# A second norm's factors brought in by TensorE with a diagonal matrix, and VectorE's boundary work in another order

## The reference

```python
def rms_norm(x, g):
    xf = x.astype(jnp.float32)
    y = xf * lax.rsqrt(jnp.mean(xf * xf, -1, keepdims=True) + EPS)
    return (y * g.astype(jnp.float32)).astype(x.dtype)

h = h + rms_norm(a, norm_g[i, 1])              # the first norm: of the block's result
f = conv_ffn(rms_norm(h, norm_g[i, 2]), ...)   # the second norm: ahead of the next block
h = h + rms_norm(f, norm_g[i, 3])
```

## Time and profile before

| | |
|---|---|
| median of three runs | 1113.65 us |
| profiled execution | 1116.95 us |
| its span | 1114.8 us |
| mean granted TensorE clock in it | 0.987 of full speed |
| TensorE matmul busy | 1056.9 us (95%) |
| VectorE busy | 681.1 us (61%) |
| ScalarE busy | 561.8 us (50%) |
| GpSimd busy | 412.9 us (37%) |

### The profile page before, as it was taken

How to read it: one execution, slowest core, us unless ns; L and a number is a source line. 1 busy time by engine, 2 the same in 40 slices (tenths; PEclk the granted TensorE clock), 3 DMA queues, 4 the chain that set the end, 5 groups by cost and what they waited for, 6 DMA issues and landing times.

```text
span 1114.8 us, 21844 instructions
## 1 busy us (share of the span) xinstructions
PE 1056.9 (95%) x8226; PEld 963.6 (86%) x8226; DVE 681.1 (61%) x1079; ACT 561.8 (50%) x1022; POOL 412.9 (37%) x283
## 2 busy tenths in 40 slices
PE   9799999999999998899999997799999999999997
PEld 7699689999978997699999967688888889999996
DVE  3555767767666656667767654567677545544444
ACT  4445565555555555465555545334434255544442
POOL 1000233343341332233343354555645355534331
PEclk9999999999999999999999998899999999999999
DMA  8234466566534442466556432133312334536551
GB/s 332 78 126 127 146 205 191 184 193 192 184 114 133 151 151 76 153 207 193 186 186 195 166 114 95 49 105 96 96 58 77 114 104 160 154 114 222 183 177 38
DMA packets 46135, 162.27 MB, mean 146 GB/s; under 512 B 5248, under 2 KB 5504, under 8 KB 45952
## 3 DMA queue, kind: packets, MB, share of 16 engines
q1 hardware_dynamic: 44784, 156.79, 43.2%
q0 software_dynamic: 1296, 4.72, 1.3%
HBM read 160.44 MB, written 1.05 MB: 145 GB/s over the span
## 4 chain that ended last, share of the span: by engine, by line
PE 83%; DVE 8%; POOL 3%; ACT 3%; issue 2%; DMA 1%; DVEq 0%; POOLq 0%; SPq 0%; ACTq 0%
PE work L388 13%; PE work L390 13%; PE work L389 13%; PE work L1590 6%; PE acc L388 5%; PE acc L389 5%; PE acc L390 5%; PE work L2299 4%; PE work L2311 2%; PE acc L2311 2%; PE acc L1839 1%; POOL low L357 1%; PE acc L1853 1%; ACT high L346 1%; PE acc L1855 1%
## 5 line engine op out<-in xcount | busy, mean ns | idle before, releaser
L357 POOL TENSOR_TENSOR low<-raw,high 128x1024 fp32r<-128x1024 f32 x109 | 264.2, 2426 | 328.9 <-ACT high L346 328.9
L357 DVE TENSOR_TENSOR low<-raw,high 128x1024 fp32r<-128x1024 f32 (+3 forms) x183 | 272.7, 1497 | 165.3 <-ACT high L346 165.2
L346 ACT ACTIVATE high<-raw 128x1024 fp32r<-128x1024 f32 (+2 forms) x293 | 300.0, 1032 | 49.3 <-DMA raw<-in_w_out 23.5
L388 PE MATMUL work<-xh,high 128*128 128x256 f32 (+1 forms) x1032 | 292.6, 283 | 0.7 <-DVE low L357 0.7
L389 PE MATMUL work<-xl,high 128*128 128x256 f32 (+1 forms) x1032 | 289.5, 280 | 0.0
L390 PE MATMUL work<-xh,low 128*128 128x256 f32 (+1 forms) x1032 | 289.0, 280 | 0.0
L388 PEld LDWEIGHTS work<-xh,high 128*128 128x128 f32 (+1 forms) x1032 | 194.6, 189 | 7.7 <-issue 4.8
L389 PEld LDWEIGHTS work<-xl,high 128*128 128x128 f32 (+1 forms) x1032 | 194.9, 189 | 2.4 <-issue 0.7
L390 PEld LDWEIGHTS work<-xh,low 128*128 128x128 f32 (+1 forms) x1032 | 194.7, 189 | 0.2
L1113 POOL TENSOR_TENSOR h<-gelu,cv 128x256 f32<-128x256 f32 x44 | 48.8, 1109 | 200.5 <-ACT gelu L1033 106.7
L1590 PE MATMUL work<-xh,high 128*128 128x256 f32 x256 | 79.1, 309 | 9.5 <-DVE silu L1639 9.5
(11 more groups left out here) (383 smaller groups left out, 2230.0 us busy)
## 6 DMA issues: line engine op xcount, KB each, us to landing
raw<-in_w_ffn SPq DMA_DIRECT2D x132, 512.0 KB, 4.3
raw<-in_w_out SPq DMA_DIRECT2D x39, 512.0 KB, 4.2
raw<-in_w_diff SPq DMA_DIRECT2D x32, 512.0 KB, 4.1
raw<-in_w_att SPq DMA_DIRECT2D x32, 512.0 KB, 3.7
raw<-in_w_gdn SPq DMA_DIRECT2D x24, 512.0 KB, 4.0
raw<-in_w_mla SPq DMA_DIRECT2D x8, 512.0 KB, 3.5
raw<-in_w_gdnz SPq DMA_DIRECT2D x8, 512.0 KB, 3.6
raw<-in_w_mla SPq DMA_DIRECT2D x8, 384.0 KB, 3.2
```

The costliest lines, as they stand in the source:

```text
L346: act.activation(high[k][:, 0:w], raw[k][:, 0:w], ACT.Copy).then_inc(high_done[k], 1)
L357: eng.tensor_tensor(low[k][:, 0:w], raw[k][:, 0:w], high[k][:, 0:w], ALU.subtract).then_inc(low_done[k], 1)
L388: pe.matmul(out, lhs[0], rhs[0], start=start, stop=False)
```

## The change

A new tensor `diag` holds, for each tile, a 128x128 matrix with the second norm's roots on the diagonal. ScalarE makes it from the identity (`pre_diag`), with the root as the scale of each row. VectorE's multiply into `hn` takes the gain alone (`pre_gained`), so it waits for `hid` and no longer for the root. TensorE multiplies `hn` by `diag` instead of transposing by the identity, which gives the transposed and scaled half at once; it takes half 0 of both tiles first, then half 1, and runs six idle products ahead instead of seven. The splits follow that order. The squares of `hid` go to `xl`. On VectorE the first norm's work stands in another order, too. At the program's beginning nothing changes.

```diff
     def pre_pe(pe, n):
         pe.wait_ge(g["const"], 48)
-        spin(pe, W[3][:], 7)
-        for t in range(NT):
-            for half in range(2):
-                pe.wait_ge(n_["hn"], 4 * (n - 1) + 2 * t + half + 1)
+        spin(pe, W[3][:], 6)
+        for half in range(2):
+            for t in range(NT):
+                pe.wait_ge(n_["hn"], 4 * (n - 1) + 2 * half + t + 1)
+                if half == 0:
+                    pe.wait_ge(n_["diag"], 2 * (n - 1) + t + 1)
                 for b in range(4):
                     at = (4 * half + b) * P
-                    last = pe.transpose(work[:, 2 * t + half, b * P:(b + 1) * P], hn[:, t, at:at + P], ident)
+                    last = pe.matmul(work[:, 2 * t + half, b * P:(b + 1) * P], hn[:, t, at:at + P], diag[:, t, :],
+                                     start=True, stop=True)
                 last.then_inc(n_["turned"], 1)
...
+    def pre_diag(act, n, t):
+        act.wait_ge(n_["root"], 2 * n + t + 1)
+        act.activation(diag[:, t, :], ident, ACT.Copy, scale=stat[:, 8 + t:9 + t]).then_inc(n_["diag"], 1)
...
-    def pre_norm(dve, n, t, half):
-        dve.wait_ge(n_["root"], 2 * n + t + 1)
+    def pre_gained(dve, n, t, half):
+        dve.wait_ge(n_["hid"], 4 * (n - 1) + 2 * t + half + 1)
...
-        dve.scalar_tensor_tensor(hn[:, t, c], hid[:, t, c], stat[:, 8 + t:9 + t], pre_gain[:, c], ALU.mult,
-                                 ALU.mult).then_inc(n_["hn"], 1)
+        dve.tensor_tensor(hn[:, t, c], hid[:, t, c], pre_gain[:, c], ALU.mult).then_inc(n_["hn"], 1)
...
     def post_dve(dve, n, p, k):
-        for t in range(NT):
-            post_gained(dve, n, t, p, k)
-            if t == 0:
-                post_mean(dve, n, 0)
-        for half in range(2):
-            post_add(dve, n, 0, half)
+        post_gained(dve, n, 0, p, k)
+        post_mean(dve, n, 0)
+        post_add(dve, n, 0, 0)
+        post_gained(dve, n, 1, p, k)
         post_mean(dve, n, 1)
+        post_add(dve, n, 0, 1)
         for half in range(2):
             post_add(dve, n, 1, half)
-            if n < 4 and half == 0:
-                pre_mean(dve, n + 1, 0)
 
     def pre_act(act, n):
         for t in range(NT):
             pre_square(act, n, t)
+        for t in range(NT):
+            pre_diag(act, n, t)
...
+    def pre_dve(dve, n):
+        pre_mean(dve, n, 0)
+        pre_gained(dve, n, 0, 0)
+        pre_mean(dve, n, 1)
+        pre_gained(dve, n, 1, 0)
         for t in range(NT):
-            pre_split_act(act, n, t)
-
-    def pre_dve(dve, n):
-        pre_norm(dve, n, 0, 0)
-        pre_mean(dve, n, 1)
-        pre_norm(dve, n, 0, 1)
-        for half in range(2):
-            pre_norm(dve, n, 1, half)
+            pre_gained(dve, n, t, 1)
```

More of the change, by code:

```diff
@@ L461, in build @@
     g = sems("g", "x second_x const")
-    n_ = sems("n", "hid sq mean root hn turned xh xl gain")
+    n_ = sems("n", "hid sq mean root diag hn turned xh xl gain")
+    diag = sb("diag", [P, NT, P])
     h = sems("h", "qkev s mx sm e p pt ptev vev pv oh ol rope roped turned turned_ev")
@@ L517, in pre_square, with pre_split_act @@
             c = cols(half)
-            act.activation(hn[:, t, c], hid[:, t, c], ACT.Square, scale=1 / 32,
+            at = 4 * t + 2 * half
+            out = xl[:, at:at + 2, :].rearrange("p b k -> p (b k)") if n else hn[:, t, c]
+            act.activation(out, hid[:, t, c], ACT.Square, scale=1 / 32,
                            accum_out=stat[:, 16 + 2 * t + half:17 + 2 * t + half]).then_inc(n_["sq"], 1)
-    def pre_split_act(act, n, t):
-        for half in range(2):
-            act.wait_ge(n_["turned"], 4 * n + 2 * t + half + 1)
-            act.activation(x_part(xh, t, half), turned(t, half), ACT.Copy).then_inc(n_["xh"], 1)
+    def pre_diag(act, n, t):
+        act.wait_ge(n_["root"], 2 * n + t + 1)
+        act.activation(diag[:, t, :], ident, ACT.Copy, scale=stat[:, 8 + t:9 + t]).then_inc(n_["diag"], 1)
+    def pre_split_act(act, n, t, half):
+        act.wait_ge(n_["turned"], 4 * n + (2 * half + t if n else 2 * t + half) + 1)
+        act.activation(x_part(xh, t, half), turned(t, half), ACT.Copy).then_inc(n_["xh"], 1)
     def pre_mean(dve, n, t):
@@ L541, in pre_split_dve @@
             for t in range(NT):
-                dve.wait_ge(n_["xh"], 4 * n + 2 * t + half + 1)
+                dve.wait_ge(n_["xh"], 4 * n + 2 * half + t + 1)
                 dve.tensor_tensor(x_part(xl, t, half), turned(t, half), x_part(xh, t, half),
@@ L612, in pre_act @@
             pre_square(act, n, t)
+        for t in range(NT):
+            pre_diag(act, n, t)
     def pre_act_split(act, n):
-        for t in range(NT):
-            pre_split_act(act, n, t)
-    def pre_dve(dve, n):
-        pre_norm(dve, n, 0, 0)
-        pre_mean(dve, n, 1)
-        pre_norm(dve, n, 0, 1)
-        for half in range(2):
-            pre_norm(dve, n, 1, half)
+        for half in range(2):
+            for t in range(NT):
+                pre_split_act(act, n, t, half)
+    def pre_dve(dve, n):
[3 more added lines that the diff above has]
+        pre_gained(dve, n, 1, 0)
+        for t in range(NT):
+            pre_gained(dve, n, t, 1)
     def boundary_act(act, n, p, k):
@@ L682, in start_act @@
         for t in range(NT):
-            pre_split_act(act, 0, t)
+            for half in range(2):
+                pre_split_act(act, 0, t, half)
         act.wait_ge(g["const"], 16)
```

## The result

The changed kernel took 1123.86 us (median of five runs, 1123.36 to 1127.13), the kernel before beside it 1115.82. The ratio over all runs is 1.0083, 95% interval 1.0070 to 1.0096: slower, by 9.3 us (the two medians lie 8.0 apart). In what follows a figure in us behind a ratio is the ratio times the median of the kernel before that ran beside it. The profiled execution took 1125.76 us with a span of 1123.6, against 1116.95 and 1114.8 before.

A forecast was written before the change was run, and what follows sets the result against it. TensorE was taken as the bound, with the change touching only four block boundaries and the last norm. Delays of 6.8 us plus 3.3 for clock falls, together 10.1, on a median of 1113.65 gave 1123.8 us; range 1118 to 1128.5.

The forecast's parts named there:

- The last add 0.71 later: First norm, first boundary: in the new order VectorE's last add ends 0.71 us later than before.
- The diagonal: Second norm, ScalarE: the 128x128 copy with a scale read per row takes 0.35 us.
- The groups: TensorE, in place of transposes: float32 products of two records, 0.23 us each, 0.92 us a group of four.
- Tile 1's multiply by the gain: VectorE, second norm: it waits for the first power and ends about 129.1; the second power ends at 129.5.
- Behind the groups: TensorE: first real product 1.00 us behind the idle product's start, as before; the changed half and tile order brings nothing.
- The sign of the 11 us: Boundaries: forecast wrong if the first real product comes less than 11 us behind the first add.
- The boundary at full clock: Four boundaries and program's end, delays alone: +1.68, +2.05, +0.56, +1.71 and +0.84, sum 6.8 us.
- The clock: TensorE's longer waits: clock falls in first and second boundary, 1.4 us each, fourth +0.5; 3.3 us.
- The total: Whole program: 6.8 us of delays and 3.3 of clock, together 10.1; median 1123.8 us; chance 0.62.
- the clock that holds: Rival, boundaries: TensorE is fast enough behind the wait; delay alone, +6 us, 1119.7 to 1120.5; chance 0.22.
- The cheap product: Rival, TensorE's groups: a product costs as little as a transpose, 0.5 us a group; no change; chance 0.05.
- the dear one: Rival, TensorE's groups: each 0.8 us more, +12 us on the delays; 1129 to 1133 us; chance 0.08.

The follow-up runs named there:

- mean_early_no_last: Kernel before with the first norm's second mean ahead of tile 0's adds, nine idle products in the fourth boundary, none behind the transposes: ratio 0.9977.
- after_spins: Changed kernel with 8, 9, 8 and 10 idle products ahead of the first group in the four boundaries, not 6: 1120.99 us, ratio 1.0060.
- order_alone: Kernel before with VectorE's new order of the first norm alone, second norm and transposes as before: 1120.47 us, ratio 1.0046.
- plain_products: Kernel before with true float32 products with the identity instead of transposes, waits and orders as before: ratio 1.0040, 4.5 us slower.
- mean_early: Kernel before with the first norm's second mean ahead of both adds of tile 0, not behind them: 1111.50 us, ratio 0.9960.

## Why the prediction was right, step by step

- **The last add 0.71 later.** Forecast 7.28 from the first gain to the last add's end; measured 7.29. The wait for the first power, the order behind it and the power that ends 0.41 behind an overlapping add came as worked out.
- **The diagonal.** Taken at 0.35, measured 0.40. The prediction's nearest row was an activation out of PSUM; a nearer one was in the same trace, of an activation from SBUF that reads a value per row too:

```profile
L2444 ACT ACTIVATE causal_prob<-causal_prob,soft 128x128 f32<-128x128 f32 x8 | 3.2, 403 | 24.2 <-DVE soft L2525 24.2
```

- **The groups.** Forecast 0.92 each, measured 0.89, in 32 records. The Trainium skill's factor of four for transpose mode ("TensorE: Matmul & The Clock Gate", "Terms") doesn't hold for start to start here: two records of 0.114 a product, against 0.145 at most for a transpose.
- **Tile 1's multiply by the gain.** The prediction lets it wait for the first power. In the kernel it waits for `hid` alone, and the three behind the second mean ran in a row from 127.82. The second power ended 9.30 behind the first gain, against 9.45 forecast.
- **Behind the groups.** The prediction took 1.00 from the idle product to the first real one, as before, and nothing for the new order of halves. From the start of the idle product to the second real product it was 1.19 before (131.01 to 132.20) and is 0.98 now (132.26 to 133.24). The 1.00 held a wait for `xl` of half 0 (mean_early_no_last), and that wait is gone: VectorE ends its last multiply earlier against the groups, and half 0 of both tiles is turned first. How much each of the two does isn't shown. This term was put at nothing and is worth 0.2 us in the first boundary, which is what separates the +1.68 forecast there from the 1.49 measured; the other differences cancel.
- **The sign of the 11 us.** The first real product was to come 11 us or more behind the first add. By its record it comes at 132.72, 10.73 behind 121.99, which is under the bound. By the end of the idle product (132.26 + 0.86 = 133.12) it is 11.13, against 11.24 forecast. I read it by the second, since its successor begins at 133.24; the bound was too near the forecast to decide anything.
- **The boundary at full clock.** Forecast +1.68, +2.05, +0.56, +1.71 and +0.84, 6.8 in all. after_spins, where the clock held, has +1.48, +1.87, +0.81, +0.71 and +0.85, 5.7; the fourth is taken against a boundary that itself had a fall (1.2 or so), without which it is +1.9, and the sum 6.9. The +0.56 of the third was wrong: it took a late product of tile 1 for a property of the kernel, and it was one of that execution. The wait ahead of its groups was 1.87 and not 1.3.
- **The clock.** Forecast were three falls of 1.4, one each in B0, B1 and B3. Three came, of 1.4 each, but one in B1 (1.42) and two in a row in B3 (2.86), and none in B0, though the wait there was 2.54 and as long as forecast (2.4). By places the forecast with the clock was 3.1, 3.5, 0.6, 2.2 and 0.8, and measured were 1.5, 3.3, 0.9, 3.6 and 0.9: the sum came out by errors on both sides, which is luck. The length of the wait ahead of the groups doesn't decide it. In these profiles no fall followed waits of 2.54 and 1.87 (B0 and B2 after), of 1.74 (B1 of order_alone) and of 1.91 (B3 of plain_products), and a fall followed 2.94, 3.11, 3.14 and 4.34, but also 1.90 (before) and 1.38 (mean_early).
- **The total.** 10.1 forecast on the execution; the places give 10.1, the span 8.8, the runs 9.3 (7.8 to 10.7). That the median, 1123.86, fell on the 1123.8 forecast is luck: the forecast started from 1113.65, and the kernel before had 1115.82 in the runs beside it.

Of the rivals, the clock that holds would have been 1119.7 to 1120.5; after_spins, which makes it hold, took 1120.99. It ran beside a kernel before of 1114.54, and by the ratio it is +6.7 where that rival had +6. The cheap product and the dear one are both refuted by plain_products. Whether transposes keep the clock up less than products, as the Trainium skill has it ("TensorE: Matmul & The Clock Gate", "Part 4: PE-mode transpose"), was not settled. For it: in the fourth boundary the clock fell over transposes behind waits of 1.38, 1.90 and 3.14 (mean_early, before, order_alone), and not over products behind 1.91 (plain_products). Against it: the second boundary of order_alone had a wait of 1.74 and 3.1 us of transposes with one wait of 0.54 among them, and stayed at 1.00. Each is one execution.

## What to carry to other kernels

Where three engines pass a value round a ring, moving a factor off one link helps only if the link that receives it has room. Here TensorE's products of 0.23 us and one more ScalarE step of 0.40 cost 0.4 to 0.6 us a boundary more than VectorE's wait had.

Before filling an engine's wait with its next job, look at what waits for the results that this delays. The new order let VectorE keep its wait for the first power and put tile 1's gain behind it, and tile 1's mean and power were on the chain. Taking that one 0.2 us mean ahead of two adds gained what the whole new method didn't.

Where a change makes the matmul engine wait longer, price the clock with it, as a likelihood and not as a certainty: here a fall over the sixteen products cost 1.4 to 1.6 us, and the changed kernel's four boundaries had none, one, none and two.

## What I had not expected

- Removing an idle product of 0.86 us from TensorE's queue, right ahead of the first real one, changed the first, second and fourth boundary by 0.02 us at most. The trace explains it: the real product was waiting for VectorE's low part all the same.
- The runs moved more than the changed places: 4.5 us against 2.2 for mean_early, 4.5 against 1.0 for plain_products. Runs of one kernel lie 1.5 to 7.1 us apart (after 1123.36 to 1127.13, at mean granted clocks of 0.987 and 0.984), and profiled executions differ outside the boundaries in where the clock falls. With one profile a kernel, the link between both isn't shown.
